# Where the rows of two modulation vectors are added: beside the attention heads instead of in the projections around them

## The reference, cut to what matters

```
mod_all = einsum('bd,lde->lbe', silu(c), ada_w) + ada_b     # 2 layers x 12288
for i in (0, 1):
    shift1, scale1, gate1, shift2, scale2, gate2 = split(mod_all[i], 6)
    h = rmsnorm(x) * (1 + scale1) + shift1
    x = x + gate1 * mixer_i(h)
    h = rmsnorm(x) * (1 + scale2) + shift2
    x = x + gate2 * (silu(h @ w1[i]) * (h @ w3[i])) @ w2[i]
return rmsnorm(x) * final_norm
```

## Time and profile before

| | |
|---|---|
| Median of three runs | 2937.81 us (2931.03 to 2937.84) |
| The profiled execution | 2924.65 us, its span 2923.0 us |
| TensorE busy | 2676.2 us, 92% of the span |
| VectorE busy | 2008.9 us, 69% |
| ScalarE busy | 1319.2 us, 45% |
| Chain that ended last | TensorE 62%, VectorE 5%, ScalarE 2%, issue 2% |
| DMA | 639.95 MB, 219 GB/s in the mean |

### The profile page before, as it was taken

The page is one execution under the profiler, slowest core; times in us unless marked ns, Lnnn a source line. Parts: engine busy times, 40 slices in busy tenths (PEclk is TensorE's granted clock), DMA queues, the critical chain, the costliest instruction groups (busy, mean ns, idle before and its releaser), DMA issues.

```text
span 2923.0 us, 55067 instructions
## 1 busy us (share of the span) xinstructions
PE 2676.2 (92%) x20605; PEld 2341.9 (80%) x20605; DVE 2008.9 (69%) x2597; ACT 1319.2 (45%) x2010; POOL 44.5 (2%) x88
## 2 busy tenths in 40 slices
PE   1299997989988999999999979988989999999998
PEld 0288886888877888888888868877878888888887
DVE  6678853788768777777777786654767755555556
ACT  1155554444444554444444444344445534444444
POOL 1000002000000000000000000000000000000000
PEclk6599999999989999999999989999989999999999
DMA  7669957443347778878788768632848855665553
GB/s 306 258 220 315 306 166 252 137 149 132 129 132 268 234 263 294 281 259 285 261 285 274 240 233 276 216 123 66 273 166 284 288 168 186 193 188 187 183 170 115
DMA packets 472654, 639.95 MB, mean 219 GB/s; under 512 B 21909, under 2 KB 427834, under 8 KB 451770
## 3 DMA queue, kind: packets, MB, share of 16 engines
q1 hardware_dynamic: 468666, 625.31, 64.0%
q0 software_dynamic: 3840, 12.59, 1.2%
HBM read 623.14 MB, written 14.68 MB: 218 GB/s over the span
## 4 chain that ended last, share of the span: by engine, by line
PE 62%; DVE 5%; issue 2%; ACT 2%; DVEq 0%; ACTq 0%
PE ps L1338 38%; PE ps L1339 19%; DVE wlo L1326 2%; PE ps L1385 1%; PE ps L1014 1%; PE ps L1005 1%; ACT whi L1321 1%; DVE ada_acc L1371 1%; DVE nt L133 1%; DVE act L146 0%; PE ps L1041 0%; PE ps L1582 0%; PE ps L1096 0%; DVE gsum L100 0%; DVE x L318 0%
## 5 line engine op out<-in xcount | busy, mean ns | idle before, releaser
L1338 PE MATMUL ps<-act,whi 128*128 128x512 f32 x3808 | 1349.4, 399 | 38.6 <-DVE act L146 16.7
L1326 DVE TENSOR_TENSOR wlo<-raw,whi 128x1024 fp32r<-128x1024 f32 (+1 forms) x768 | 901.7, 1192 | 496.7 <-ACT whi L1321 493.4
L1339 PE MATMUL ps<-act,wlo 128*128 128x256 f32 x3808 | 1071.5, 281 | 0.0
L1321 ACT ACTIVATE whi<-raw 128x1024 fp32r<-128x1024 f32 (+1 forms) x768 | 773.9, 1030 | 649.6 <-PE ps L1339 647.5
L1338 PEld LDWEIGHTS ps<-act,whi 128*128 128x128 f32 x3808 | 723.3, 190 | 214.1 <-DVE wlo L1326 23.7
L1338 PE MATMUL ps<-hid,whi 128*128 128x512 f32 x2176 | 776.9, 399 | 11.8 <-DVE wlo L1326 8.8
L1339 PEld LDWEIGHTS ps<-act,wlo 128*128 128x128 f32 x3808 | 727.1, 191 | 0.0
L1339 PE MATMUL ps<-hid,wlo 128*128 128x256 f32 x2176 | 616.5, 283 | 0.0
L1338 PEld LDWEIGHTS ps<-hid,whi 128*128 128x128 f32 x2176 | 414.7, 191 | 112.8 <-DVE wlo L1326 11.6
L1339 PEld LDWEIGHTS ps<-hid,wlo 128*128 128x128 f32 x2176 | 413.8, 190 | 0.0
L1371 DVE SCALAR_TENSOR_TENSOR ada_acc<-ada_ring,sc,ada_acc 128x2048 f32<-128x2048 f32 x128 | 300.3, 2346 | 0.3
(11 more groups left out here) (272 smaller groups left out, 2266.1 us busy)
## 6 DMA issues: line engine op xcount, KB each, us to landing
raw<-in_f_w SPq DMA_DIRECT2D x480, 512.0 KB, 4.6
ada_ring<-in_ada_w SPq DMA_DIRECT2D x172, 1024.0 KB, 7.4
raw<-in_a_w_rkv SPq DMA_DIRECT2D x96, 512.0 KB, 5.0
raw<-in_b_w_in SPq DMA_DIRECT2D x56, 512.0 KB, 4.0
raw<-in_f_w SPq DMA_DIRECT2D x64, 384.0 KB, 3.9
first_ring<-in_ada_w SPq DMA_DIRECT2D x20, 1024.0 KB, 5.3
raw<-in_a_w_o SPq DMA_DIRECT2D x32, 512.0 KB, 6.6
raw<-in_b_w_o SPq DMA_DIRECT2D x32, 512.0 KB, 6.0
```

Source lines behind the costliest of these rows:

```text
L1321: self.nc.scalar.activation(self.whi[:, u % SPL, 0:n], self.raw[:, u, 0:n], ACT.Copy).then_inc(self.s("hi_ready"), 1)
L1326: self.nc.vector.tensor_tensor(self.wlo[:, u % SPL, 0:n], self.raw[:, u, 0:n], self.whi[:, u % SPL, 0:n].bitcast(F32), SUB).then_inc(self. ...
L1338: self.nc.tensor.matmul(o, hi[:, kk, c0:c1], src[:, k].rearrange("p a t -> p (a t)"), start=k == 0, stop=False)
L1339: last = self.nc.tensor.matmul(o[:, T:2 * T], lo[:, kk, c0:c1], src[:, k, 0, :], start=False, stop=k == ktotal - 1)
```

## The change

Rows 148 to 159 (the last of piece 9) are no longer added in the first layer's last down projection and the first pairs of the projection, but in pairs 1 to 6 of the projection. Piece 9 is summed and finished at the end of `IndexKey`. Rows 160 to 175 (piece 10) are added in the heads, two in each round, at the end of VectorE's round, and loaded at the end of SyncE's round. Their memset stands ahead of the rounds, and piece 10 is finished in the first pair of the output projection, which adds no rows any more. TensorE waits for piece 9's `mod_ready` ahead of the heads' first matmul, since both use the same PSUM bank. Row by row: 8 additions fewer in the down projection, 12 instead of 14 in the projection, 16 instead of none in the heads, none instead of 6 in the output projection.

```diff
@@ IndexKey.__init__
         self.n = 2 * 136
+        self.rows, prog.rows_done = prog.take_piece(prog.rows_done), None
@@ IndexKey.vector
         p.nc.vector.tensor_tensor(p.kiw[:], p.ps[:, 4:6, 0:T], p.small_beside_proj[:, 0], ADD).then_inc(p.s("kiw"), 1)
+        p.ada_finish(dve, *self.rows)
@@ IndexKey.tensor
             p.multiply(u, 2, 2 * u, KT, 136, ((0, P), (8, 136)), p.act, (4, 5)).then_inc(p.s("unit_used"), 1)
+        p.ada_sum(pe, *self.rows)
@@ Attention.__init__
         self.units = prog.split_units
+        self.rows = 160
+        prog.rows_done = 10
@@ Attention.sync, inside the loop over i
                 sp.dma_start(A[j]["uv"][:], ...).then_inc(s(f"uv_loaded{j}"), 16)
+            for j in range(2):
+                p.ada_stream(sp, self.rows, i, j)
@@ Attention.vector
         dve.wait_ge(s("barred"), 2)
 
+        p.ada_zero(dve)
         with dve.Fori(0, self.n) as i:
...
                 nc.vector.tensor_tensor(p.hid_lo[:, m, :], ...).then_inc(s("o_lo"), 1)
+                p.ada_add(dve, self.rows, i, j)
@@ Attention.tensor
+        p.mod_wait(pe, 9)
         for n, c in enumerate((4, 0, 1, 2, 3)):
@@ Program.build
         phases += self.ffn(0, [[(0, 4, 88), (4, 8, 96)], [(0, 4, 104)], [(0, 8, 112)], [(0, 4, 128)],
-                               [(0, 4, 136), (4, 6, 144)], [(0, 4, 148)]], dsa_in)
-        phases.append(Linear(self, dsa_in, 7, dsa_tail, self.act, Normed(self, 6, 7), ToProj(self), [(0, 2, 156), (2, 7, 160)]))
+                               [(0, 4, 136), (4, 6, 144)], ()], dsa_in)
+        phases.append(Linear(self, dsa_in, 7, dsa_tail, self.act, Normed(self, 6, 7), ToProj(self), [(1, 7, 148)]))
...
-        phases.append(Linear(self, b_w_o, 4, self.ffn_first(1), hid, None, AddGated(self, 8, True), [(0, 3, 170)], ready=heads))
+        phases.append(Linear(self, b_w_o, 4, self.ffn_first(1), hid, None, AddGated(self, 8, True), ready=heads))
```

## The result

The changed kernel takes 2980.85 us (median of four runs, 2969.07 to 2990.08) against 2934.42 us (2926.27 to 2937.84) for the kernel before in the same session. The ratio is 1.0157, with a 95% interval from 1.0131 to 1.0184: slower by 46 us. The profiled execution took 2979.49 us with a span of 2977.7 us, 54.7 us more than the span before. Lines of `kernel.py` behind the change stand about ten further down than before (L1007 is the turn of `uk` that was L997).

What follows compares the result with a forecast made beforehand. TensorE was taken as busy most of the span, with room on VectorE and DMA in the heads. Costs of 59.5 us less gains of 11.7 made 47.8 us more: 2972 us, plus 13 for the median, 2986 us (2975 to 3000).

Steps and rivals of the forecast that it cites:

- Part 1: First layer's last down projection: losing its eight row additions gains 6.6 us, the difference from the second layer's same stage.
- Part 2: Projection: losing piece 9's sum gains 5.1 us; its row additions, and the output projection's, lie under matmuls and gain nothing.
- part 3: End of the index key: piece 9's sum and handoffs, 4.4 us less TensorE's 2.4 us idleness, cost 2.0 us.
- Part 4: Ahead of the heads: the accumulator's memset comes before lgf on VectorE's path and costs 1.8 us (bounds 0 and 1.8).
- Part 5: Heads' rounds: VectorE's two additions cost 1.4 us in the last round and 3.9 us ahead of the output projection.
- Part 6: Heads: in SyncE's queue uk stands behind a row waiting for an addition; TensorE stalls 7.0 us in each of six rounds.
- the clock: Heads: after each stall TensorE's granted clock is halved for a while, costing 1.4 us a round in six rounds.
- Which rounds pay: Heads: the first turn waits for nothing added there and the last round turns nothing, so six rounds pay, 50.4 us.
- (A): Rival: uk still comes before TensorE needs it, only VectorE's lateness counts, 2935 to 2943 us; chance 0.09.
- (B): Rival: transfers do not queue behind each other, so six rounds cost 35 us in place of 50, 2970 us; chance 0.12.
- (C): Rival: transfers queue as badly as the weight unit, so six rounds cost 73 us, 3009 us; chance 0.12.
- (D): Rival: the change does not do what it says, the heads' rows being added elsewhere; given no chance.

Runs made afterwards that it cites:

- experiment 1: The changed kernel with SyncE issuing the next round's uk and uv ahead of the round's two rows: 2929.87 us, ratio 0.9998; run again 2925.86 us, 0.9986.
- experiment 5: The kernel before, with the eight row additions of its last down projection cut to 128 columns, loads whole: 2928.37 us, ratio 0.9985.
- experiment 4: The changed kernel with rows in the heads both loaded and added at 128 columns only, order, waits and memset kept: 2925.27 us, ratio 0.9988.
- experiment 6: The changed kernel with SyncE's order turned round, memset behind piece 9's finish, one addition per round ahead of the low parts: 2927.40 us, ratio 0.9979.
- experiment 3: The changed kernel with each addition in the heads cut to 128 of 2048 columns, loads whole: 2954.51 us, ratio 1.0101.
- experiments 2: The changed kernel with each row loaded in the heads cut to 128 columns, additions, waits and order kept: 2960.63 us, ratio 1.0115.

## Why the prediction was right

Forecast were 47.8 us more and 2986 us in all (2975 to 3000); measured were 46.4 us more and 2980.85 us. Of the 5 us between the two times 3.4 are the kernel before, whose median was 2934.42 us beside this run and not 2937.81. The cause, SyncE's order, was forecast and is shown by experiment 1; how closely the sum is met is in part luck, as the parts show.

**Part 1** (gain 6.6 us, bounds 0 and 18.8). Measured 7.5 us in the traces. The second layer's own stage was the right yardstick, and experiment 5 shows that the additions cause it. Its size was 0.9 us too small as the second layer's distance was itself 73.0 us in the execution before and 72.13 in the one after.

**Part 2** (5.1 us) **and part 3** (2.0 us). Together -3.1 us were forecast and -4.3 measured. In the projection no pair of lines stands further apart any more; the twelve steps between its first thirteen L95 lines are 11.29 to 11.37 us each, though VectorE adds two rows in most of them (two of the lines):

```profile
1796.67 0.58 ACT L95 ACTIVATE small_beside_proj<-ps 128x512 f32<-128x512 f32 x1
1807.99 0.57 ACT L95 ACTIVATE small_beside_proj<-ps 128x512 f32<-128x512 f32 x1
```

At the index key the sum stands where part 3 put it, and the heads' first matmul waits for nothing but VectorE's addition:

```profile
1911.74 3.63 PE L1395 MATMUL ps<-ones,ada_acc 128*128 128x1 f32 x32
1915.63 4.19 PE L984 MATMUL ps<-tmp,ones 128*128 128x256 f32 x10 [0.27 <-DVE mod L1403]
```

That is 3.9 us from the sum's start to the heads, less the 2.4 of idleness before: 1.5 us against 2.0. The rest of the difference is pace. The earlier trace rows shows 1.6 us lost to the clock ahead of the index key before, and after the same stretch has a clock of 1.00. Against that, the first four steps of the projection, 11.09 us each before, take 11.31 after (see below): 0.9 us more. The sum -5.1 + 1.5 - 1.6 + 0.9 = -4.3 us is what was measured. The 0.7 us of pace has no term in the forecast.

**Part 4** (1.8 us). The memset stands on VectorE's path exactly as said:

```profile
1942.90 0.41 DVE L947 TENSOR_SCALAR barr<-wrk 128x128 f32<-128x128 f32 x2
1943.81 1.76 DVE L1374 MEMSET ada_acc<- 128x2048 f32 x1 [0.49 <-DVE barr L947]
1945.89 0.56 DVE L956 TENSOR_TENSOR lgf<-ps,barr 128x384 f32<-128x384 f32 x1 [0.32 <-DVE ada_acc L1374]
```

But the stretch was +3.7 us, not +1.8. To the first round's start it is 2.7 us longer, at a granted clock of 0.80 and 0.82 where before it was 0.89 and 1.00. That is not the memset: the kernel of experiment 1 took 24.25 us for it in one execution and 26.85 in another (24.18 before, 26.84 after). The first round itself is 13.55 us in place of 12.56. TensorE, late by its clock, hid part of the memset. Where it was not late (experiment 1's first execution) the memset cost more: TensorE waited 1.61 us for the first `prf` and the first round took 14.81 us. In experiment 4 the same wait was followed by a mean granted clock of 0.75 for the rest of the round, which took 16.28 us. With the memset moved away (experiment 6) the first round took 12.55. So the memset's price is 1.0 to 2.3 us, and 3.7 where the clock falls behind it. The term of 1.8 lies in that, and its upper bound of 1.8 was too low.

**Part 5** (1.4 in the last round and 3.9 behind it). Measured 4.6 us of 5.3. Experiment 3 shows that the additions are this cost: with them at 0.34 us the way out was 11.94 us again, the 11.86 of before. The last round was 0.9 us late and not 1.4: its `lgf` started at T + 1.8, before at T + 0.95. The exit had a second price that the prediction put at nothing, the slow first 6 us of the output projection (1.2 us, above). In the other rounds VectorE's lateness costs nothing, as forecast at the low end: experiment 1 has rounds of 12.48 us.

**Part 6** (7.0 us a round) **and the clock** (1.4). Measured 6.4 later at the turn, and 1.95: 8.35 us a round against 8.4, six times 50.1 us against 50.4. The mechanism is the one that was forecast, but that the sum is met to 0.3 us is luck: one term was 0.6 us too large and the other 0.55 too small.

The landing was forecast well. SyncE issued the second row at 1979.95, D + 0.2 (D is 1977.43 + 2.34 = 1979.77 in this round), and it took 4.9 us, so it landed at D + 5.1 (forecast D + 5.0). `uk`, issued at 1980.83, took 4.7 us and landed at D + 5.8 (forecast D + 5.7):

```profile
ada_ring<-in_ada_w SPq DMA_DIRECT2D x1, 1024.0 KB, 4.9
...
uk<-in_b_w_uk SPq DMA_DIRECT2D x1, 256.0 KB, 4.7
```

That SyncE issued `uk` at D + 1.06 and not at D + 0.55 does not show in its landing: it came 0.7 us behind the second row, which is the forecast's own term. What was off is D: it came 1.9 us behind T and not 2.3. The round's first low part starts 3.37 us ahead of the next T in both kernels (1995.31 and 1998.68; 2025.88 and 2029.25 in the earlier trace rows), but an addition starts 0.34 us behind the start of its low part (0.42 us long), and a low part 2.26 us behind that of an addition (2.34 us long). They overlap a little, where the forecast had put a gap of 0.05 us between them. The remaining 0.2 us had been set down for the second head's `uk`, and TensorE does not wait for it ahead of the turn.

The prediction also gave the landing by the formula that the Trainium skill states for loads issued by GpSimd ("DMA: Bandwidth & Descriptors", anatomy of one DMA, SWDGE path), while these loads are issued by SyncE. By it, an estimate, a row takes 4.4 us and `uk` lands at D + 5.1. Here a row took 4.9 us and `uk` landed at D + 5.8, so the price read from the rows was the nearer one.

The clock was the step that was off most in relation to its size: 1.95 us for 1.4. The turn and the keys run slow for longer than the 3.1 us that the earlier trace rows show, as the window rows above say: 0.50 for 3.5 us, then a mean of 0.74 for 3.6. The rule of the Trainium skill ("TensorE: Matmul & The Clock Gate", on loop structure) that a wait for a DMA in the loop drops the clock to half agrees with the 0.50. Its other half, that a copy by VectorE behind the matmuls does not, no run here shows; a wait of 6.96 us with no DMA at its end, ahead of the output projection, was followed by a clock of 0.50 as well.

**Which rounds pay** was right: a first round of 13.55 us, then six of 20.5 to 21.9, and no stall in the last.

**The rivals.** (A) The hold doesn't bite: refuted, `uk` is issued at D + 1.06. Its forecast of what the time would be without the hold, 2935 to 2943 us for a kernel before of 2938, or -3 to +5 us, is near what experiment 1 shows when the hold is taken away (by its two ratios -0.6 and -4.1 us). (B) `uk` passes the rows: refuted in its mechanism, for the turn starts as soon as 2.66 and 2.83 us after its issue only where the rows are small (experiments 2 and 4). (C) It queues as a weight unit does, 9.0 us: refuted, 4.7. (D) is refuted by the rows in the heads.

## What to carry to other kernels

When an operation is moved onto an engine, look at the load that feeds it and at what is written behind that load in the issuing queue. A wait in that queue is paid by every later load, and a load that used to go out 11 us early can come 6 us late though all engines and the DMA have room. Turning round the order of the two loads, with the same work and the same traffic, gave back all of 50 us. And a long addition behind a round's last result costs the next stage's start; it belongs where its engine waits anyway.

## What the runs showed that was not expected

**Matmuls at a granted clock of 1.00 run at two paces.** A group of the projection took 11.09 us in the first four steps of the trace before (two of its L95 lines), and 11.31 us from 1809.95 on the earlier trace rows.

```profile
1771.35 0.58 ACT L95 ACTIVATE small_beside_proj<-ps 128x512 f32<-128x512 f32 x1
1782.45 0.58 ACT L95 ACTIVATE small_beside_proj<-ps 128x512 f32<-128x512 f32 x1
```

After the change all full steps are 11.31, in experiments 4 and 6 all are 11.09. Experiment 1's kernel had 11.31 in its first profiled execution and 11.09 in its second, with nothing changed. That is 2%, or 2.8 us in this stage alone, and it may be part of why the runs of one kernel spread by 10 us and more. What sets it is open.

**The low clock falls in different places.** From the heads' first matmul to the first turn the kernel of experiment 1 took 15.78 us at a granted clock of 0.89 once and 17.11 us at 0.80 the other time.

**The landing time depends on the company.** With the order turned round a round's `uv`, rows and `uk` go out in this order within 4.7 us, and both rows within 1.0 us (the issues of one such round):

```profile
ada_ring<-in_ada_w SPq DMA_DIRECT2D x2, 1024.0 KB, 8.2
uk<-in_b_w_uk SPq DMA_DIRECT2D x2, 256.0 KB, 8.9
```

and in the kernel after, where the wait puts 2.6 us between the rows:

```profile
ada_ring<-in_ada_w SPq DMA_DIRECT2D x2, 1024.0 KB, 4.9
uk<-in_b_w_uk SPq DMA_DIRECT2D x2, 256.0 KB, 4.9
```

So `uk` takes 8.9 us in the version that has no stall and 4.9 in the one that stalls. It is issued 3.0 us behind T there too, but it is the one for the next round's turn: it lands at T + 11.9 and is needed at T + 13.8. The repaired order has 1.9 us to spare, no more.
